# A two-layer encoder on one core: seven products in another order, no barrier between the layers, low parts of the weights on VectorE, a new opening and end

## What is computed

```python
for layer in range(DEPTH):                      # DEPTH = 2, x is (1024, 1024)
    h = rms_norm(x, norm_g[layer])
    z = h @ w_in[layer]                         # 1024 x 4864
    qa, ka, va, ga, qr, kr, vr, gr, gm = split_columns(z)
    qa, ka = rope(rms_norm(qa)), rope(rms_norm(ka))
    ya = (silu(ga) * block_attention(qa, ka, va)) @ w_branch_attn[layer]
    qr, kr = rope(qr), rope(kr) * RET_HEAD_DIM ** -0.5
    orr = head_group_norm(bidirectional_retention(qr, kr, vr, lg_f, lg_b))
    yb = (silu(gr) * orr) @ w_branch_ret[layer]
    gates = sigmoid(gm)
    x = x + (gates[0] * ya + gates[1] * yb) @ w_out[layer]
return rms_norm(x, final_norm_g)
```

## Time and profile before

| | us |
|---|---|
| median of 3 runs | 1934.1 (1932.88 to 1935.05) |
| the profiled execution's own time | 1931.47 |
| its span, first to last instruction | 1929.7 |
| TensorE matmul busy | 1812.3 (94%) |
| VectorE busy | 1061.7 (55%) |
| GpSimd busy | 836.7 (43%) |
| ScalarE busy | 668.2 (35%) |
| mean granted TensorE clock | 0.988 |

### The profile page before, as it was taken

How to read it: one execution, slowest core, us unless ns; L and a number is a source line. 1 busy time by engine, 2 the same in 40 slices (tenths; PEclk the granted TensorE clock), 3 DMA queues, 4 the chain that set the end, 5 groups by cost and what they waited for, 6 DMA issues and landing times.

```text
span 1929.7 us, 32806 instructions
## 1 busy us (share of the span) xinstructions
PE 1812.3 (94%) x10784; PEld 1590.6 (82%) x10784; DVE 1061.7 (55%) x2246; ACT 668.2 (35%) x1564; POOL 836.7 (43%) x652
## 2 busy tenths in 40 slices
PE   3899989999999999999878998999999999999995
PEld 3788978899999888888667887789999988888874
DVE  6979678635554210107977987794444541110478
ACT  4368438622212100003433872683222210000133
POOL 3348337623422323335823773485223422323383
PEclk9999999999999999999989999999999999999998
DMA  7100000101111111124130001001011111112132
GB/s 248 33 12 13 27 23 23 45 23 44 35 30 34 44 55 44 44 65 164 34 124 23 23 1 49 9 15 45 24 43 43 44 33 44 44 54 65 50 136 88
DMA packets 129593, 96.40 MB, mean 50 GB/s; under 512 B 15664, under 2 KB 114224, under 8 KB 129456
## 3 DMA queue, kind: packets, MB, share of 16 engines
q1 hardware_dynamic: 125920, 84.56, 14.1%
q10 hardware_dynamic: 3536, 10.17, 1.5%
HBM read 82.13 MB, written 12.58 MB: 49 GB/s over the span
## 4 chain that ended last, share of the span: by engine, by line
PE 69%; DVE 16%; issue 6%; DMA 3%; ACT 2%; POOL 2%; DVEq 1%; SPq 1%; ACTq 0%; POOLq 0%
PE ps L566 17%; PE ps L568 17%; PE ps L567 17%; PE ps L701 5%; PE ps L690 4%; DVE xh L1711 3%; PE ps L714 2%; PE ps L716 2%; DMA xh<-xs 2%; PE ps L807 2%; DVE pT_lo L1477 1%; PE ps L791 1%; DVE zqk L1388 1%; DVE rtb L1396 1%; DVE hT_lo L1698 1%
## 5 line engine op out<-in xcount | busy, mean ns | idle before, releaser
L566 PE MATMUL ps<-w_hi,hT_hi 128*128 128x256 f32 (+1 forms) x1280 | 390.3, 305 | 13.9 <-DVE hT_lo L1343 9.3
L568 PE MATMUL ps<-w_hi,hT_lo 128*128 128x256 f32 (+1 forms) x1280 | 376.5, 294 | 0.0
L567 PE MATMUL ps<-w_lo,hT_hi 128*128 128x256 f32 (+1 forms) x1280 | 376.3, 294 | 0.0
L383 POOL TENSOR_SCALAR w_hi<-raw 128x1024 fp32r<-128x1024 f32 x100 | 108.4, 1084 | 398.5 <-PE ps L568 368.4
L566 PEld LDWEIGHTS ps<-w_hi,hT_hi 128*128 128x128 f32 x1280 | 245.0, 191 | 17.4 <-issue 12.5
L566 PE MATMUL ps<-hT_hi,w_hi 128*128 128x512 f32 x640 | 254.6, 398 | 0.0
L567 PE MATMUL ps<-hT_lo,w_hi 128*128 128x512 f32 x640 | 251.1, 392 | 0.0
L568 PE MATMUL ps<-hT_hi,w_lo 128*128 128x512 f32 x640 | 250.8, 392 | 0.0
L567 PEld LDWEIGHTS ps<-w_lo,hT_hi 128*128 128x128 f32 x1280 | 245.2, 192 | 0.3
L568 PEld LDWEIGHTS ps<-w_hi,hT_lo 128*128 128x128 f32 x1280 | 244.6, 191 | 0.0
L389 POOL TENSOR_TENSOR w_lo<-raw,w_hi 128x1024 fp32r<-128x1024 f32 x84 | 207.5, 2470 | 6.0
(11 more groups left out here) (175 smaller groups left out, 3543.0 us busy)
## 6 DMA issues: line engine op xcount, KB each, us to landing
raw<-w_in SPq DMA_DIRECT2D x168, 256.0 KB, 3.2
xs<-xh SPq DMA_DIRECT2D x2, 4096.0 KB, 17.6
xh<-xs SPq DMA_DIRECT2D x8, 1024.0 KB, 13.9
xh<-x ACTq DMA_DIRECT2D x4, 1024.0 KB, 10.1
raw<-w_a SPq DMA_DIRECT2D x16, 256.0 KB, 2.9
raw<-w_r SPq DMA_DIRECT2D x16, 256.0 KB, 3.2
w<-w_o SPq DMA_DIRECT2D x4, 1024.0 KB, 11.6
ctA<-rope_a SPq DMA_DIRECT2D x8, 256.0 KB, 2.9
```

The source lines that it names most:

```text
L383: nc.gpsimd.tensor_scalar(place(pos)[0], raw[:, slot], 1.0, 1.0, ALU.mult, ALU.mult).then_inc(w_rounded, 1)
L566: nc.tensor.matmul(outp, ah, bh, start=(start and i == 0), stop=False)
L567: nc.tensor.matmul(outp, ah, bl, start=False, stop=False)
L568: last = nc.tensor.matmul(outp, al, bh, start=False, stop=(stop and i == len(pairs) - 1))
```

## The change

The order of the seven products is new: what were products 3, 4, 5 are now 5, 3, 4, and the tables, the slots of their left operands (`A_SLOT`) and the places of the right ones (`IN_W`) follow. All fourteen `right_lo` instructions of a layer go from GpSimd to VectorE; the left sums of products 5 and 6 go from VectorE to GpSimd.

The last product is taken tile by tile (`last_product`), and inside it TensorE turns the next layer's tiles 0 and 1. VectorE's list there is `add_up(4)`, mean square, `norm_x` 0 and 1, `add_up(5)`, `lo_x` 0 and 1, `add_up(6)`, `norm_x` 2. No `phase_end` stands at the border; single waits replace it.

In the opening the first half row of `x` comes from two queues, SyncE's and ScalarE's, ahead of the constants; ScalarE and VectorE make the first three units of weights themselves (`first_hi`, `first_lo`); ScalarE squares whole rows (`square_row`), the first two ahead of the tile loop and two more in each of its steps 0 to 2; VectorE has mean squares of tile 0, of 1, of 2 and 3, and of 4 to 7; the decays are computed inside the tile stage, in three pieces. At the end VectorE writes the normed tiles 0 to 3 before `add_up(5)`, and the last four with two mean squares. The loop over the layers, and SyncE's loops, are written out.

```diff
-LEFT = (((1, 0, 1),), ((0, 0, 1), (0, 1, 1)), ((0, 0, 1), (1, 0, -1)), ((1, 0, 1), (1, 1, 1)),
-        ((1, 0, 1), (0, 1, 1)), ((0, 1, 1),), ((1, 1, 1), (0, 1, -1)))
+LEFT = (((1, 0, 1),), ((0, 0, 1), (0, 1, 1)), ((0, 0, 1), (1, 0, -1)), ((1, 0, 1), (0, 1, 1)),
+        ((0, 1, 1),), ((1, 0, 1), (1, 1, 1)), ((1, 1, 1), (0, 1, -1)))
...
+                def last_product(p):
...
+                    for i in range(4):
+                        pe.wait_ge(o_post, base + POSTS[p - 2] + len(INTO[p - 2]) * (i + 1))
...
+                        if L + 1 < DEPTH and i >= 1 and i <= 2:
+                            pe.wait_ge(o_post, base + POSTS[p - 1] + len(INTO[p - 1]) * (2 * i))
+                            turn_x(i - 1, L + 1)
...
+                    for t in range(T):
...
                         outputs(t)
+                        if j == 0 and L == 0:
+                            if t < 3:
+                                square_row(2 + 2 * t)
+                                square_row(3 + 2 * t)
...
-                        norm_x(L, 2)
+                        first_lo(2)
+                        mean_square(1, 2, 2, 12)
+                        norm_x(0, 1)
                     for t in range(T):
                         if j == 0 and t + 1 < T:
-                            lo_x(t + 1)
+                            if L == 0 or t > 0:
+                                lo_x(t + 1)
+                            if L == 0 and t < 2:
+                                if t == 0:
+                                    mean_square(2, 4, 4, 24)
+                                norm_x(0, t + 2)
                             if t == 1:
-                                mean_square(L, 1)
+                                mean_square(4, 8, SQ0(L + 1) if L == 0 else SQ0(L) + N_SQ, 36 if L == 0 else NW_0 + L * NW_L + 12)
...
+                        if j == 0 and L == 0:
+                            if t == 2:
+                                decays_start()
+                            if t == 4:
+                                decays_ratio()
+                            if t == 6:
+                                decays_end()
...
                 left_sum(1)
                 left_lo(1)
+                right_lo(1)
+                left_sum(3)
                 add_up(0)
-                left_sum(3)
+                right_lo(2)
                 left_lo(3)
                 add_up(1)
-                left_sum(4)
+                right_lo(3)
                 left_lo(4)
                 add_up(2)
+                right_lo(4)
+                right_lo(5)
                 left_lo(5)
                 add_up(3)
-                left_sum(6)
                 left_lo(6)
+                right_lo(6)
                 add_up(4)
...
+                if L + 1 < DEPTH:
...
+                    norm_x(L + 1, 0)
+                    norm_x(L + 1, 1)
+                    add_up(5)
+                    lo_x(0, L + 1)
+                    lo_x(1, L + 1)
+                    add_up(6)
+                    norm_x(L + 1, 2)
+                else:
+                    for t in range(4):
+                        norm_out(t)
+                    add_up(5)
+                    add_up(6)
```

More of the change, by code:

```diff
@@ L334, in _ @@
                         unit(i % 2, n0 + (i - 1 if i else 0), cols(i % 2, L, c0 + h * RD))
-                with sp.Fori(0, K // 2) as mm:
+                for mm in range(0, K // 2):
                     n0 = u0 + U_D1 + mm * (2 * N_D1)
@@ L368, in _ @@
                 x_block(1, 0)
-            for t in range(1, T, 2):
-                put_out(sp, t)
-            sp.wait_ge(out_done[1], 16 * (T // 2))
+            for t in range(T):
+                if t not in OUT_ACT:
+                    put_out(sp, t)
+            sp.wait_ge(out_done[0], 16 * (T - len(OUT_ACT)))
         @block.gpsimd
@@ L1311, in _ @@
-            half = DEPTH * RH
-            for c in range(6):
-                a = (c % 2) * half
-                ins = V.tensor_scalar(dec[:, :, c], lgw[:, 2, a:a + half], icol[:, c:c + 1], None, ALU.mult)
-                if c == 5:
-                    step(ins)
-                else:
-                    ins.then_inc(pro_dve, 1)
-                    done[0] += 1
-            assert done[0] == 22, done
-            mean_square(0, 0)
-            dve.wait_ge(gain_in, 16)
-            norm_x(0, 0)
@@ L1324, in _, with decays_start @@
[L1324 to L1329 removed]
+            dec_half = DEPTH * RH
+            def decays_start():
+                dve.wait_ge(consts_in, NCONST)
+                step(V.tensor_scalar(lgw[:, 1], lgw[:, 0], -1.0, None, ALU.mult))
+                step(V.tensor_tensor(lgw[:, 1], lgw[:, 1], lgw[:, 0], ALU.min))
@@ L1332, in _, with lo_x @@
                 dve.sem_inc(s, 1)
-            dve.drain().then_inc(phase_end, 1)
-            with dve.Fori(0, DEPTH) as L:
-                dve.wait_ge(phase_end, 3 + L * PH_L)
-                def lo_x(t):
+            V.memset(ss4[:, T:], 0.0).then_inc(a_zero, 1)
+            dve.wait_ge(a_zero, 1)
+            mean_square(0, 1, 1, 0)
+            dve.wait_ge(gain_in, 16)
+            norm_x(0, 0)
+            first_lo(0)
+            first_lo(1)
+            for L in range(DEPTH):
+                def lo_x(t, L=L):
                     for hf in range(2):
@@ L1714, in _, with right_lo @@
                     merge(b)
+                def right_lo(p):
+                    if p == 0:
+                        dve.wait_ge(o_blo, L * (2 * N_P) + 2 * N_P)
+                    for h in range(2):
+                        dve.wait_ge(o_bhi, L * (2 * N_P) + 2 * p + h + 1)
+                        hi, lo = right_slot(p, h)
+                        V.tensor_tensor(lo, right_src(p, h), hi.bitcast(F32), ALU.subtract).then_inc(o_blo, 1)
                 left_sum(2)
```

356 lines of the change are left out of this document (210 added, 146 removed).

## The result

The changed kernel takes 1946.6 us (median of 4 runs, 1945.6 to 1948.2) against 1934.6 for the kernel before (4 runs): the ratio is 1.0064, 95% interval 1.0047 to 1.0082. It is slower by 12 us, as forecast (1946), though not for every reason that the forecast gave. That two wrong terms of the forecast nearly cancelled is luck. The profiled execution took 1948.2 us, with a span of 1945.2 and a mean granted clock of 0.981.

A forecast was written before the change was run, and what follows sets the result against it. It took TensorE to be dense, waiting on the opening's barrier and on VectorE, which paces the tile stage. Opening 10, border -4, end 7 made 13 us over 1931.5; adjusted towards the median, forecast 1946, range 1923 to 1957.

The forecast's parts named there:

- The opening, +10: Start through tile projections: a 12.5 us lead is lost behind late squares and added decays; stage ends 10 us later.
- 36.9 of 40: Tile stage, 60 to 100 us: VectorE busy 36.9 of 40 us, so it sets the pace and added work is paid.
- the rival that the lead is kept: Opening: the 12.5 us lead stays through VectorE slack or timely ScalarE rows, rest as forecast; 1924 us, chance 0.10.
- The decays, 4.3 + 0.9: Tile stage: decay arithmetic moved from idle to full VectorE costs 4.3 us more, and `decays_end` 0.9.
- The products, no gain: Seven products, first layer: VectorE's longer list, blocked by GpSimd's sums, leaves no gain in the products themselves.
- The rival in which GpSimd's sums do not block VectorE: Products: five to six blocks of 2.2 us vanish, 17 gained at border, 3 at end; 1924 us, chance 0.13.
- The border, 4 gained: Between layers: TensorE stops 8 us inside product 6, yet projection starts at 977.0, not 979.64; 4 us gained with clock.
- the mean square 961.3, `hb` 0 and 1 at 964.4: Border, VectorE: after squares end at 958.9, the mean square ends at 961.3 and both row products at 964.4.
- the bound at 0: Border: gain falls to 0 if the fills' port use delays `hb` as before (5.27 us for two).
- The end, +7: After the last products: product 5's add and a second mean square join the final chain; 7 us lost.
- The code written out, 0 with 3 gained as its end: Layer loops written out: adds no busy instruction, priced at 0, with 3 us as the gain's other end.
- the argument that TensorE's waits name only 1.2 us of issue: Whole span: TensorE's waits show just 1.2 us of issue, so writing the code out was priced at 0.

The follow-up runs named there:

- Experiment 1: Changed kernel with ScalarE's squares of tiles 2 to 7 put ahead of the outputs of tile 0: 1928.9 us.
- kernel 10: Changed kernel with squares early, product 5's add before the mean square, right low parts on GpSimd, fills held, decays moved just ahead of first attention: 1907.0 us.
- experiment 2: Changed kernel with the decays' arithmetic moved from the tile stage to the start of the first layer's second head group: 1947.6 us.
- Experiment 3: Changed kernel with product 5's add ahead of the mean square of the left rows, in both layers: 1938.3 us.
- experiment 5: Kernel before the change, with only its layer loop and SyncE's inner loops written out: 1927.3 us, ratio 0.9969.
- kernel 11: Changed kernel: squares early, product 5's add first, right low parts on GpSimd, decays before first attention, fills held from the second weight unit: 1903.3 us.

## Why the prediction was right, and where it was not

The sign and the time came out (1946.0 forecast, 1946.6 measured), but two terms were wrong by 6 to 7 us each, in opposite senses. The sign rests on the opening and the end, whose mechanisms were right; that the time is met within a microsecond is luck.

- **The opening, +10: right in size, +11.6.** Its chain came as written: squares behind `outputs`, waits of TensorE ahead of tiles 2 and 4 of 7.0 and 6.9 us (7 to 7.5 said), `lo_x(3)` at 52.8 (54.8 said). The first turn came at 10.5 rather than 9.1, because the gains landed later, and the lead was 11.8 us rather than 12.5. Experiment 1 shows the cause by taking it away. What failed is a step beside it, the use of "36.9 of 40" against the rival that the lead is kept: with squares early 6.3 us of the lead are kept, which is nearly all of it less the 5.3 of the decays, and with the decays elsewhere too (kernel 10) 11.7. That VectorE is busy 36.9 of 40 us says that work added there is paid for, which held; it does not say that an earlier start is lost, since VectorE had been idle 7 of the 31.8 us ahead of that window.
- **The decays, 4.3 + 0.9: right**, 5.3 us by experiment 2 (6.5 in kernel 10).
- **The products, no gain: right, nearly row by row.** Shifted by 10.3 us the list put the add of product 4 at 961.2 to 966.1; it ran from 960.1 to 965.0. Product 6 was put at 963.3 and began at 962.4. (Three products in 33.67 us are 11.2 each and not 11.1, which changes nothing.) The rival in which GpSimd's sums do not block VectorE is refuted by the pairs of 4.55 us above.
- **The border, 4 gained: wrong.** The projection starts 84.3 us behind the landing of `xh` (993.88 and 909.59), where 77.7 were forecast and the kernel before took 80.3. The third stretch is 2.6 longer, and 4.9 longer than in the kernel before with its layers written out. The step that failed is "the mean square 961.3, `hb` 0 and 1 at 964.4": 2.4 and 3.1 us. The 2.4 are taken from the opening, where the first fill began only behind the mean square, at 19.3. They took 8.8 and 4.7. The stop of 8 us inside product 6 became 15.8; with the fills held it is 7.2. The prediction named this effect only as the bound at 0, for `hb` alone, though the kernel before had it in the mean square as well (960.62 to 966.08, 5.5 us; its lines stand above).
- **The end, +7: right**, 6.0. The last output was to end 86.0 us behind the landing and ended 85.1 behind it. Experiment 3 shows that it is the order: product 5's add ahead of the outputs brings back 5.7.
- **The code written out, 0 with 3 gained as its end: wrong**, 6.3 gained by experiment 5, of which the changed kernel shows 1.3 in its second stretch and perhaps 2.4 in its fourth. The step that failed is the argument that TensorE's waits name only 1.2 us of issue: the time was gained all the same. Where it stood, no row shows.

So the sum that was 10 - 4 + 7 was by the traces 11.6 + 2.6 + 6.0 - 3.7, and 12 by the medians. The 2.6 and the 3.7 both hold a part of the gain from the written-out code.

## What to carry to other kernels

When an opening is made shorter, follow the first wait that the new order puts behind somebody else's product: six squares of 1.3 us, placed behind outputs that wait for TensorE, cost 16 to 18 us. In a chain of tiny VectorE steps beside GpSimd work on SBUF, a step that meets a GpSimd instruction lasts until that one ends (up to 2.2 us for 0.16); holding GpSimd back for a moment can be worth as much as a reordering on VectorE (8.5 us here, against 8.3), until what GpSimd makes becomes the next wait. And a full window shows that added work is paid for, not that an earlier start is wasted: look whether the engine was idle ahead of it, take its input earlier and look again.

## What the runs showed of the hardware

- A VectorE step of 128x4 takes 0.16 us alone and up to 2.2 beside a GpSimd subtraction of 128x1024 (2.34 to 2.41 us); twelve such steps took 2.4 us without fills and 8.8 with them. A step that reads one tensor only is held up as well (2.29 us in kernel 11). The Trainium skill, SBUF — State Buffer, section SBUF: two separate sides, says that GpSimd and a VectorE instruction with two SBUF inputs, or in a two-port mode, share a pair of ports that is held for a whole instruction, so that the other blocks fully; the rows agree, down to the length of a step.
- Adds whose one operand is in PSUM took 0.61 us each (4.86 for eight) beside GpSimd's sums as without them: they were not blocked.
- With the layers written out, the kernel before is 6.3 us faster (0.3%), with the same instructions in the same order on each engine apart from the loops' branches and the register arithmetic of the waits.
